# Attention by two heads of a tile at a time in a decoder step

## The reference, cut to what is computed here

```python
H_ATT, DH_ATT = 8, 64          # attention heads
H_MEM, DH_MEM, N_MEM = 4, 128, 256   # cross attention into 256 memory tokens

def sparse_core(q, k_sel, v_sel, valid):      # over the keys that the indexer chose
    s = jnp.einsum("bthd,btkhd->bthk", q, k_sel) * (DH_ATT ** -0.5)
    s = jnp.where(valid[:, :, None, :], s, -jnp.inf)
    p = jax.nn.softmax(s, axis=-1)
    return jnp.einsum("bthk,btkhd->bthd", p, v_sel)

def mem_attend(qm, mk, mv):
    s = jnp.einsum("bthd,bmhd->bthm", qm, mk) * (DH_MEM ** -0.5)
    p = jax.nn.softmax(s, axis=-1)
    return jnp.einsum("bthm,bmhd->bthd", p, mv)
```

## Time and profile before

| | |
|---|---|
| median of 3 runs | 2982.36 us (2980.09 to 2985.59) |
| the profiled execution | 2974.08 us, its span 2972.5 us |
| PE busy | 2844.4 us (96%) |
| PE weight loads | 2709.4 us (91%) |
| VectorE, ScalarE, GpSimd busy | 2341.1 us, 1236.1 us, 1137.3 us |
| DMA | 340.35 MB, mean 114 GB/s |

### The profile page before, as it was taken

One profiled execution on the slowest core, in us unless ns is written; L12 is line 12 of the kernel. 1 busy time (PEld: TensorE's weight loads), 2 busy tenths in 40 slices (PEclk: granted clock), 3 DMA queues, 4 the chain that ended last, 5 costly groups with the idle time before them and its releaser, 6 DMA issues. The chain is left out here.

```text
span 2972.5 us, 56828 instructions
## 1 busy us (share of the span) xinstructions
PE 2844.4 (96%) x21242; PEld 2709.4 (91%) x21242; DVE 2341.1 (79%) x3873; ACT 1236.1 (42%) x2373; POOL 1137.3 (38%) x808
## 2 busy tenths in 40 slices
PE   6999989999999999999988999999989999899999
PEld 6999989999899999999986777799889999899999
DVE  8888897777758999999985666547378888977776
ACT  5444444444433333233445555521344443443443
POOL 4555545554543331113321000021355555454552
PEclk8999999999999999999998999999999999999999
DMA  4333323332232222223128777634533333233331
GB/s 160 93 93 93 104 75 93 93 92 87 86 80 87 87 87 75 85 58 95 59 89 298 265 238 253 227 121 137 148 101 99 100 93 101 75 103 98 95 98 57
DMA packets 359407, 340.35 MB, mean 114 GB/s; under 512 B 16831, under 2 KB 293666, under 8 KB 359134
## 3 DMA queue, kind: packets, MB, share of 16 engines
q1 hardware_dynamic: 354430, 330.41, 35.9%
q0 software_dynamic: 4128, 4.20, 0.5%
q10 hardware_dynamic: 576, 2.10, 0.2%
HBM read 299.60 MB, written 37.05 MB: 113 GB/s over the span
## 5 line engine op out<-in xcount | busy, mean ns | idle before, releaser
L294 PE MATMUL bank<-op_r_ffn,w_hi 128*128 128x256 f32 (+1 forms) x2992 | 580.8, 292 | 32.4 <-DVE op_r_ffn L275 18.2
L294 PEld LDWEIGHTS bank<-op_r_ffn,w_hi 128*128 128x128 f32 x2992 | 475.5, 191 | 39.1 <-issue 36.5
L294 PE MATMUL bank<-op_r_ffn,w_lo 128*128 128x256 f32 (+1 forms) x1496 | 433.5, 290 | 0.0
L294 PE MATMUL bank<-h_hi,w_hi 128*128 128x362 f32 (+1 forms) x1272 | 422.2, 332 | 6.8 <-ACT qi L2024 2.6
L435 POOL TENSOR_TENSOR w_lo<-sums_ffn,w_hi 128x512 fp32r<-128x512 f32 x214 | 317.7, 1494 | 264.5 <-ACT w_hi L431 264.5
L294 PE MATMUL bank<-h_lo,w_hi 128*128 128x362 f32 (+1 forms) x1272 | 417.9, 329 | 0.0
L294 PE MATMUL bank<-h_hi,w_lo 128*128 128x362 f32 (+1 forms) x1272 | 417.8, 328 | 0.0
L294 PE MATMUL bank<-op_r_ffn,more_hi_ffn 128*128 128x288 f32 (+1 forms) x1936 | 375.0, 291 | 13.9 <-ACT s_ffn L575 5.3
L294 PEld LDWEIGHTS bank<-op_r_ffn,more_hi_ffn 128*128 128x128 f32 x1936 | 306.3, 190 | 17.8 <-issue 8.5
L435 POOL TENSOR_TENSOR more_lo_ffn<-sums_ffn,more_hi_ffn 128x512 fp32r<-128x512 f32 x138 | 203.2, 1480 | 226.4 <-ACT more_hi_ffn L431 226.4
L294 PEld LDWEIGHTS bank<-op_r_ffn,w_lo 128*128 128x128 f32 x1496 | 286.0, 191 | 0.0
(11 more groups left out here) (429 smaller groups left out, 7141.8 us busy)
## 6 DMA issues: line engine op xcount, KB each, us to landing
raw<-in_w_ffn_in SPq DMA_DIRECT2D x132, 512.0 KB, 3.9
raw_ffn<-in_w_ffn_out SPq DMA_DIRECT2D x88, 512.0 KB, 3.5
v_ring<-in_cache_v SPq DMA_DIRECT2D x128, 256.0 KB, 4.7
raw<-in_w_in SPq DMA_DIRECT2D x53, 512.0 KB, 4.9
raw_ffn<-in_w_ffn_in SPq DMA_DIRECT2D x44, 512.0 KB, 3.8
kt_two<-in_cache_k SPq DMA_DIRECT2D x88, 256.0 KB, 3.6
kept_g<-stage SPq DMA_DIRECT2D x24, 544.0 KB, 3.1
gate<-kept_g SPq DMA_DIRECT2D x24, 544.0 KB, 3.7
```

The costliest lines, as they stand in the source:

```text
L294: mm = pe.matmul(out, left, right, start=(start and i == 0 and j == 0), stop=(stop and i == n - 1 and j == 2))
```

## The change

The 96 jobs become 48 "doubles": the same tile of two heads (2hp, 2hp+1), or two tiles of one memory head. 12 steps now make up two samples, and each step has up to three places for the samples' entries.

- Scores: q_high, q_low, k_high, k_low hold a pair of heads, each head on its own 64 partitions. For a chunk of keys there are three products (high·high, high·low, low·high), each as two instructions, one per head, at `tile_position` (0, 0) and (64, 0), into two banks. A double takes banks 0 to 3.
- Values: 64 columns of values are stationary, at `tile_position` (0, 0) or (0, 64), and the 128 columns of transposed probabilities move. The output has the 64 + 64 dimensions of both heads in its rows, 128 queries in its columns: it is transposed already, and the oturn transposes with their evictions go. Memory values likewise, with 256 moving columns.
- The inverse sums have to stand by columns too: VectorE takes both reciprocals at once, spreads them over 64 (or 128) columns each (`invert`), TensorE transposes that (`inverse`), it is evicted to inv_t, and VectorE multiplies bank 6 by it into qT or qmT.
- In step d the list has scores d, values d-2, turns d-1, invert d-1, exponential d, inverse d-1.
- The splits run once per pair, on 128 partitions. pb has two buffers instead of three, pt holds 16 blocks instead of 8, vp one buffer instead of two.
- Turns use banks 4 and 7 in the steps of wide tiles (4 to 7), and 4, 7, 1, 3 in the others.

```diff
-    slots = [
-        [],
-        [("sc", 0)],
-        ...
-        [("pt", 0), ("pt", 1), ("pt", 2), ("pt", 3), ("pt", 4)],
-        [("pv",), ("mpt",)],
-        [("mpv",), ("ot",)],
-        [("mot",)],
-        [],
-    ]
+    slots = [
+        ([], [], [("sc", 0)]),
+        ([("sc", 1)], [], [("sc", 2)]),
+        ([("sc", 3)], [], [("sc", 4), ("smax",)]),
+        ([], [], [("soft",), ("msc",)]),
+        ([("pt", 0), ("pt", 1), ("pt", 2)], [("pt", 3), ("pt", 4)], [("pv",), ("mpt",)]),
+        ([("mpv",)], [("ot",)], [("mot",)]),
+    ]
...
+    for d in range(n + 2):
+        if d < n:
+            add(d, "scores", d)
...
+        sample(d, 0)
+        if 0 <= d - 2 < n:
+            add(d, "values", d - 2)
+        if n <= d:
+            add(d, "merge", 2 + 2 * (d - n))
+        sample(d, 1)
+        if 0 <= d - 1 < n:
...
+                add(d, "turn", d - 1, g, min(4, blocks - g))
+            add(d, "invert", d - 1)
+        if d < n:
+            add(d, "exp", d)
+        sample(d, 2)
+        if 0 <= d - 1 < n:
+            add(d, "inverse", d - 1)
...
-                        pe.matmul(out, qq[:, i * P:(i + 1) * P], kk_hi[:, k0:k0 + w], start=True, stop=False)
-                        mm = pe.matmul(out, qq[:, i * P:(i + 1) * P], kk_lo[:, k0:k0 + w], start=False, stop=True)
+                        if c:
+                            for t in held_at[d].values():
+                                wait_turn(pe, t)
+                        for m, (q_, k_) in enumerate(((q_hi, k_hi), (q_hi, k_lo), (q_lo, k_hi))):
+                            for e in range(2):
+                                r = slice(e * DH, (e + 1) * DH)
+                                mm = pe.matmul(bank[2 * e + c][:, 0:w], q_[r, i * P:(i + 1) * P], k_[r, k0:k0 + w],
+                                               start=(m == 0), stop=(m == 2), tile_position=(e * DH, 0))
...
-                    for j in range(i + 1):
-                        mm = pe.matmul(bank[6][:, 0:DH], pt[:, j, :], vp[:, h // 2 % 2, j, h % 2 * DH:(h % 2 + 1) * DH],
-                                       start=(j == 0), stop=(j == i))
+                    for j in range(i + 1):
+                        for e in range(2):
+                            r = slice(e * DH, (e + 1) * DH)
+                            mm = pe.matmul(bank[6][r, 0:P], vp[:, j, r], pt[:, e * (i + 1) + j, :], start=(j == 0),
+                                           stop=(j == i), tile_position=(0, e * DH))
...
-            elif kind == "oturn":
-                pe.wait_ge(normed, s + 1)
-                o = o_sb[:, 4 * entry[2]:4 * entry[2] + 4, :] if jobs[s][0] == "att" else o_m
-                for q in range(4):
-                    mm = pe.transpose(tb[:, q * P:(q + 1) * P], o[:, q, :], ident[:, :])
+            elif kind == "inverse":
+                d = s
+                pe.wait_ge(spread, d + 1)
+                for e in range(1 if doubles[d][0] == "att" else 2):
+                    mm = pe.transpose(tb[:, e * P:(e + 1) * P], inv[:, e, :], ident[:, :])
...
+            elif kind == "invert":
+                dve.wait_ge(exped, 2 * d + 2)
+                if d >= 1:
+                    dve.wait_ge(turned, turn_of[("inverse", d - 1)] + 1)
+                dve.reciprocal(rinv[:, c:c + 2], rsum[:, c:c + 2]).then_inc(inverted, 1)
+                dve.wait_ge(inverted, d + 1)
...
+                dve.wait_ge(valued, d + 1)
+                wait_turn(dve, turn_of[("inverse", d)])
+                dve.tensor_tensor(to, bank[6][:, 0:w], inv_t[:, :, :].rearrange("p e n -> p (e n)")[:, 0:w], ALU.mult).then_inc(normed, 1)
```

More of the change, by code:

```diff
@@ L2827, in attention_plan, with add @@
     turns = 0
-    def add(*entry):
+    def add(step, *entry):
         nonlocal turns
         turn = None
-        if entry[0] in ("turn", "oturn", "pt", "mpt", "ot", "mot"):
+        if entry[0] in ("turn", "inverse", "pt", "mpt", "ot", "mot"):
             turn = turns
             turns += 1
[L2835 to L2858, removed]
-            for g in range(0, blocks, 4):
[L2860 to L2870, removed]
@@ L2871, in attention_plan, with sample @@
-    return jobs, plan
+        plan.append((entry, turn, step))
+    def sample(d, place):
+        if d < n:
+            for e in slots[d % 6][place]:
+                add(d, e[0], d // 6, *e[1:])
+    n = len(doubles)
+    add(0, "queries", 0)
+    add(0, "keys", 0)
+    for d in range(n + 2):
+        if d < n:
+            add(d, "scores", d)
+            following = d // 12 + 1
+            if d % 12 == 8 and following < H // 2:
+                add(d, "queries", following)
+            if d % 12 == 9 and following < H // 2:
+                add(d, "keys", following)
+        sample(d, 0)
[5 more added lines that the diff above has]
+        if 0 <= d - 1 < n:
+            blocks = 2 * (doubles[d - 1][1] + 1) if doubles[d - 1][0] == "att" else 4
+            for g in range(0, blocks, 4):
+                add(d, "turn", d - 1, g, min(4, blocks - g))
+            add(d, "invert", d - 1)
+        if d < n:
+            add(d, "exp", d)
+        sample(d, 2)
+        if 0 <= d - 1 < n:
+            add(d, "inverse", d - 1)
+        if d == n - 1:
+            add(d, "merge", 0)
+            add(d, "merge", 1)
+        elif d == n:
+            add(d, "merge", 3)
@@ L2916, in attention, with wide @@
     st = mem.at("st", [P, 8], F32, AT_C + 3552)
     table = mem.at("table2", [1, DEC_B * PAGES], I32, AT_C + 3584)
-    last_third = max(turn for entry, turn in plan if turn is not None and entry[0] == "turn" and entry[1] < len(jobs) - 6)
+    def wide(d):
+        return d < n and d % 12 in (1, 3, 5, 7)
     bank_of, before = [], []
     held = {}
-    for turn in range(sum(turn is not None for _, turn in plan)):
-        free = (4, 7, 1) if turn <= last_third else (4, 7)
+    held_at = {}
+    for entry, turn, step in plan:
+        if entry[0] == "scores" and wide(step):
+            held_at[step] = {b: held[b] for b in (1, 3) if b in held}
+        if turn is None:
+            continue
+        free = (4, 7) if wide(step) or step < 2 or step >= n - 3 else (4, 7, 1, 3)
@@ L3138, in on_pe @@
         after_heads(pe, "mem_keys_normed")
-        for entry, turn in plan:
+        values_there = False
+        for entry, turn, step in plan:
             kind, s = entry[0], entry[1]
@@ L3309, in on_act @@
     def on_act(act):
-        for entry, turn in plan:
+        for entry, turn, _ in plan:
             kind, s = entry[0], entry[1]
```

376 lines of the change are left out of this document (184 added, 192 removed).

## The result

The changed kernel takes 2990.74 us, the kernel before in the same runs 2979.56 (medians of 20 runs each; ratio 1.0035, 95% interval 1.0027 to 1.0042). It is 0.35% slower. The forecast was 2977.5, which is 2 us less than this median of the kernel before and 5 less than the 2982.4 that it started from. The time lies inside the range given, on the side that had a chance of 0.23.

What follows compares the result with a forecast made beforehand. PE was taken to bound the attention stage; work -25.2, first key pages +4.5 and new waits +15.3 gave -5, so 2977.5 us against the 2982.4 median; range 2961 to 2993.

Steps and rivals of the forecast that it cites:

- the side that had a chance of 0.23: Whole kernel: slower than before by more than the 6 us that a measurement can tell, chance 0.23.
- First key group: Attention stage's first 20 us: PE waits some 5 us for the fourth key group's pages, +4.5 net.
- New waits: PE waiting for VectorE's inverse: 22 us over four pairs, less 6.7 of old waits before the values, +15.3.
- Step 9: Step 9 of each pair's twelve: PE waits about 3 us for the inverse, the worst place.
- step 3: Step 3 of each pair's twelve: PE waits about 1 us for the inverse.
- Shapes on PE: PE's tile shape changes 277 times instead of 192; 85 more at 0.18 us each, +15.3.
- cheap changes of shape: Bound where a tile-shape change costs one side only: 7.7 us in all, PE's work falling 33 instead of 25.
- Values and scores: PE's products with two heads side by side: values -31.7 us, scores -8.8 us.
- End: Stage's end, last sample's values to first merge product: 10.8 us, ended by a late weight, nothing saved there.
- The slower rival: Attention stage: the chain of one double at a time becomes the bound, +10.6 us, 2993, chance 0.16.
- None of the three signs: Forecast wrong if scores or values exceed single passes, idle before two-head scores passes 10 us, or inverse idle stays under 12.

Runs made afterwards that it cites:

- filler: Changed kernel plus 232 unread identity transposes on PE ahead of the waiting inverses; 2981.87 us, ratio 1.0009 to before.
- Spread with filler: Changed kernel with sample key-group scores set further apart and unread identity transposes ahead of the waiting inverses, 6 more at double 0; 2971.64 us, ratio 0.9970.
- Filler at the pages too: Changed kernel with unread identity transposes ahead of the inverses and 14 (36 in the first sample) ahead of each fourth key group's scores; 2980.69 us, ratio 1.0003.
- the spread: Changed kernel with the sample's key-group scores set further apart: first three earlier, fourth behind its step's values; 2976.53 us, ratio 0.9991 to before.
- constant inverse: Changed kernel with PE's inverse transposing a constant, without waiting for VectorE, result not the reference's; 2991.84 us, ratio 1.0043 to before.
- `sc 3`: Sample scores of the fourth key group; by itself: changed kernel with only these moved behind their step's values; 2984.02 us, ratio 1.0018 to before.
- late splits: Both splits of the next pair moved from double 9 to 10: over the changed kernel 2989.31 us (1.0033), with sample scores also set further apart 2970.38 us (0.9961).

## Why the forecast was wrong

Idle time and own work of PE in the stage, from the profiles:

| us | before | changed | difference | forecast |
|---|---|---|---|---|
| idle of PE | 27 | 60 | +33 | +20 |
| its work, falls of the clock about as before | 302 | 269 | -33 | -25 |
| the clock's falls beyond those of before | | 12 | +12 | none |
| stage | 329.5 | 341.2 | +11.7 | -5 |

That work comes from the two kernels with filler at nearly full clock. Spread with filler: 323.4 less 26 idle less 256 transposes of 0.11 make 269. Filler at the pages too: 332.6 less 24 less 366 of 0.11 make 268. In the changed kernel 341.2 less 60 leave 281, 12 more. The clock's records say the same by another way: half of the time in which PE was busy at 1.2 GHz is lost, so 15.9 us of the 31.8 after and 4.4 of the 8.8 before, 11.5 more. (The two kernels with filler still lose 3.5 and 2.2.)

The clock failed by 12 us and the waits by 13; the changes of shape were priced 8 too dear, which hid a part of it.

- **The clock has no term in the sum.** This is the first step that failed: put at nothing without a reason, it cost 12 us. The prediction read the granted clock (0.98) and took it as given; its waits were priced at their own length. In the earlier trace rows it had 0.95 for the first 20 us, a stretch with waits. Two runs bear the price out: filler gives 9 us back over the changed order, 5 over the spread.
- **First key group, 4.5.** This is the second step that failed. The wait of the first sample was 4.53 (with both of its ends late). Wrong is that it was priced once: of the seven samples behind it six wait 0.8 to 1.9 for a group, 9 us. The prediction worked out the landing of one group and didn't ask when its place in the ring is freed in the steady state. The spread, which frees it earlier, took 14 us off the kernel, the falls of the clock that went with it included.
- **New waits, 15.3.** Step 9 was right to 0.1 us, and step 3 too (0.99; 1.65 in the first pair). A pair in the middle waits 0.9, 1.0, 0.7, 2.9 and 1.2, so 6.7 for the 5.5 assumed, and the stage's last inverse waits 2.69: 28.0 for 22. Of the old waits not 6.7 but 13.7 went, the memory values' 7.0 too. So the term came to 14.3, near its 15.3, but by luck: both of its parts were off by 6 or 7.
- **Shapes on PE, +15.3.** That work fell by 33, which is the bound with cheap changes of shape (33), not 25. By this remainder a change costs about 0.09, not 0.18; no run changes the number of changes alone. From rows 3 the gap at a change and the uncovered load were added up, and the runs don't say which of them is the one.
- **Values and scores, -31.7 and -8.8.** Right, from start to start.
- **End.** From the last sample's values to the first merge product were 10.8 us and are 12.3; 3.9 for w_lo and 2.7 for the inverse stand in it.

The slower rival named about this time (+10.6), but by another way: waits of 9 us a pair before the scores. There are none (0.0 and 1.3 us before the scores of attention and memory). It was the right size with the wrong mechanism, and its chance (0.16) was no insight. The chain that it names does stand behind the inverse: with the constant inverse 4.0 and 7.4 us of idle appear at the scores.

None of the three signs that were to show the forecast wrong appeared: no group took longer than its single passes at 2.4 GHz, nothing waited before the scores, and the inverse's idle is over 12. A sign on the granted clock was missing.

What is not settled: why the same wait of 2.94 brings a fall two times of three, in both orders; why three waits of 1 us bring one in the changed order and none with the spread; and what share of the spread's gain `sc 3` has by itself.

## What to carry to other kernels

When a change takes work from the bounding engine and leaves it waits, ask twice: is each wait priced in the steady state, not only where it is seen first, and does PE's clock hold behind it. Read the clock row by row beside the waits before a sum is made. An edit that only moves a wait is worth nothing until the wait that paces is gone: late splits gave nothing that can be told over the changed order and 6 us after the spread. The version to keep is two heads at a time with the spread and the late splits, 2970.4 us, 0.9961 of before.

## What the runs showed of the hardware

- PE's granted clock fell to 1.2 GHz ten times in the stage, for some microseconds each: behind two of three waits of 2.94 us, behind one of 1.85, and in three places behind three waits of about 1 us that stand close together. Twelve transposes of 1.47 us then took 2.02 to 2.79. Work that nobody needs, put in the place of the waits, halved the number of falls (five) and made this kernel 9 us faster.
- Two tiles of 64 columns side by side take 0.11 a pass for 128 moving columns, as one alone, and two of 64 rows take 0.24 for 512 columns of the split halves, as one of 128 rows. No part of the gain is lost for two.
